# RMS norm factors applied behind the products: gated projection, latent attention and final rows of a two-layer decoder step

## The reference, cut to what matters

```python
def rmsnorm(x, g):
    y = x * rsqrt(mean(x * x, axis=-1) + EPS)      # one factor per token
    return y * g                                   # one gain per channel

# layer 0
h = h + conv_module(rmsnorm(h, g_mix[0]))
h = h + hier_moe(rmsnorm(h, g_ffn[0]), ...)        # 32 experts, two per token
h = ple_add(h, p[0], g_ple[0], ...)
c    = rmsnorm(rmsnorm(h, g_kv_in) @ w_dkv, g_lat) # shared latent, 256 wide
k_pe = rope(rmsnorm(h, g_kv_in) @ w_kr)            # 32 wide
# layer 1
cq = rmsnorm(rmsnorm(h, g_mix[1]) @ w_dq, g_q)     # 384 wide
h  = h + attention(cq, c, k_pe, cache) @ w_o
h  = h + hier_moe(rmsnorm(h, g_ffn[1]), ...)
h  = ple_add(h, p[1], g_ple[1], ...)
y  = rmsnorm(h, g_final)

def ple_add(h, p, g, w_gate, b_gate, w_proj):
    gate = sigmoid(rmsnorm(h, g) @ w_gate + b_gate)  # 1024 x 1024
    return h + gate * (p @ w_proj)                   # 256 x 1024
```

## Time and profile before

| | |
|---|---|
| median of 3 runs | 1585.22 us (1583.94 to 1587.91) |
| profiled execution | 1589.59 us, its span 1587.7 us |
| PE busy | 1201.2 us, 76% of the span |
| DVE busy | 499.3 us, 31% |
| ACT busy | 264.5 us, 17% |
| POOL busy | 58.9 us, 4% |
| mean granted TensorE clock | 0.861 of full speed |
| DMA moved | 477.03 MB |

### The profile page before, as it was taken

The page is one execution under the profiler, slowest core; times in us unless marked ns, Lnnn a source line. Parts: engine busy times, 40 slices in busy tenths (PEclk is TensorE's granted clock), DMA queues, the critical chain, the costliest instruction groups (busy, mean ns, idle before and its releaser), DMA issues. The chain is left out here.

```text
span 1587.7 us, 23342 instructions
## 1 busy us (share of the span) xinstructions
PE 1201.2 (76%) x10176; PEld 781.7 (49%) x10176; DVE 499.3 (31%) x1326; ACT 264.5 (17%) x643; POOL 58.9 (4%) x46
## 2 busy tenths in 40 slices
PE   6978897865866855579898897989776676675586
PEld 4846664433433532347675554855443343343265
DVE  2792512112112112132575664151111111111143
ACT  1162221100100100011223432022000010010011
POOL 0340000000000000000200100000000000000000
PEclk9989998877877877789999998899787787887898
DMA  5953269999999998995213342629999999999930
GB/s 155 296 213 137 106 270 422 418 423 420 418 423 419 419 423 325 416 346 127 106 46 142 132 168 107 258 108 419 422 419 420 422 418 421 421 419 419 418 128 28
DMA packets 91279, 477.03 MB, mean 300 GB/s; under 512 B 21676, under 2 KB 32841, under 8 KB 73230
## 3 DMA queue, kind: packets, MB, share of 16 engines
q1 hardware_dynamic: 89188, 456.34, 71.5%
q0 software_dynamic: 1792, 18.88, 3.2%
q10 hardware_dynamic: 186, 0.20, 0.0%
HBM read 473.37 MB, written 2.49 MB: 300 GB/s over the span
## 5 line engine op out<-in xcount | busy, mean ns | idle before, releaser
L880 PE MATMUL ps<-area,hiddenT 128*32 128x256 f32 x2112 | 201.9, 547 | 236.6 <-issue 223.5
L880 PEld LDWEIGHTS ps<-area,hiddenT 128*32 128x32 f32 x2112 | 92.4, 148 | 319.8 <-issue 299.4
L1452 DVE COPY y<-ps 32x256 f32<-32x256 f32 x128 | 53.3, 417 | 471.9 <-PE ps L880 471.0
L870 PE MATMUL ps<-area,uT 128*32 128x256 f32 x2176 | 148.3, 432 | 42.1 <-DMA area<-in_w_exp_up_dram 27.9
L870 PEld LDWEIGHTS ps<-area,uT 128*32 128x32 f32 x2176 | 84.6, 127 | 105.3 <-issue 44.1
L870 PE MATMUL ps<-area,xsT 128*32 128x256 f32 x2048 | 134.9, 420 | 0.0
L1160 PE MATMUL ps<-sel,u_rows 128*128 128x256 f32 (+3 forms) x480 | 123.6, 384 | 0.0
L1408 ACT COPY y<-ps 32x256 f32<-32x256 f32 x128 | 46.7, 364 | 431.4 <-PE ps L880 430.6
L870 PEld LDWEIGHTS ps<-area,xsT 128*32 128x32 f32 x2048 | 82.6, 126 | 55.3 <-issue 25.7
L1498 DVE TENSOR_TENSOR hidden<-silu,ps 128x128 f32<-128x128 f32 x64 | 18.4, 287 | 266.4 <-ACT silu L1420 266.4
L1160 PEld LDWEIGHTS ps<-sel,u_rows 128*128 128x128 f32 (+1 forms) x480 | 75.7, 188 | 40.7 <-issue 31.8
(11 more groups left out here) (325 smaller groups left out, 1278.6 us busy)
## 6 DMA issues: line engine op xcount, KB each, us to landing
area<-in_w_exp_gate_dram SPq DMA_DIRECT2D x66, 2048.0 KB, 27.1
area<-in_w_exp_up_dram SPq DMA_DIRECT2D x66, 2048.0 KB, 30.6
area<-in_w_exp_down_dram SPq DMA_DIRECT2D x66, 2048.0 KB, 26.1
area<-in_conv_w_in_dram SPq DMA_DIRECT2D x8, 1024.0 KB, 12.7
area<-in_w_ple_gate_dram SPq DMA_DIRECT2D x2, 4096.0 KB, 35.8
area<-in_conv_w_out_dram SPq DMA_DIRECT2D x1, 4096.0 KB, 19.3
area<-in_w_o_dram SPq DMA_DIRECT2D x1, 4096.0 KB, 14.2
area<-in_w_uq_dram SPq DMA_DIRECT2D x3, 768.0 KB, 12.2
```

The source lines that it names most:

```text
L870: last = pe.matmul(s.ps[SLOT * j:SLOT * (j + 1), bank, 0:2 * P].rearrange("p (a f) -> p a f", a=2), xT[:, k, :], up[:, :, k, j * P:(j + 1) ...
L880: last = pe.matmul(s.ps[SLOT * g:SLOT * (g + 1), bank, 0:q], hidden[:, SLOT * j:SLOT * (j + 1)], down[:, j, g * q:(g + 1) * q], start=(j = ...
L1452: last = V.tensor_copy(y[a:a + SLOT, (e // PER) % 2, g * q4:(g + 1) * q4], s.ps[SLOT * g:SLOT * (g + 1), 3 + e % 2, 0:q4])
```

## The change

1. Norm factors behind the products. For the gate product of `ple_stage`, the latent, rotary and query products of `mla_stage` and the final rows, only the gain is applied before the product, by ACT (`Copy` with a scale per partition). The factor per token is multiplied onto each product's result by DVE. For the final rows the gained chunks are turned into rows first and the factor, turned too, is applied as a scale per partition while the rows are copied out.
2. Chunk by chunk. Gain and square of a chunk follow the add that completes it in `hT`: those for the gate product behind the last `combine` within the experts' block, those of the next norm behind each chunk of the gate, with the sum of squares (and in layer 1 the transposes) placed on PE between the gate products.
3. The per-layer products `p @ w_proj` move into experts 28 to 31, two chunks per expert, copied by ACT into `m.proj`, which takes the room of `u_rows`. Squares and gained chunks lie in the room of the down slots.
4. `final_stage` is gone; its work stands in layer 1's `ple_stage`. The output goes out in three DMAs, one of them issued by ACT. `w_ple_proj` has a semaphore of its own.

The diff, cut to its core (the loops of ACT and DVE over the chunks of `ple_stage` are whole):

```diff
 # experts_stage, PE
+                def project(c):
+                    if c == 0:
+                        pe.wait_ge(s.ple_proj_in.sem, s.ple_proj_in.at(16))
+                    else:
+                        pe.wait_ge(s.ple_out.sem, s.ple_out.at(c))
+                    for k in range(PLE // P):
+                        last = pe.matmul(s.ps[:, 5, 0:T], ple_weights(s)[1][:, k, c * P:(c + 1) * P],
+                                         s.pT[:, layer, k, :], start=(k == 0), stop=(k == PLE // P - 1))
+                    last.then_inc(s.ple_mm.sem, 1)
...
+                    if e >= CUT:
+                        project(2 * (e - CUT))          # behind the transpose of expert e
...
+                    if e >= CUT:
+                        project(2 * (e - CUT) + 1)      # behind its down product
 # experts_stage, ACT, behind the last expert
+                for c in range(DC):
+                    act.wait_ge(s.added.sem, s.added.at(DC * (quads - 1) + c + 1))
+                    gain = VEC["g_ple"] + DC * layer + c
+                    nc.scalar.activation(s.uT[:, c, :], s.hT[:, c, :], ACT.Copy, scale=s.vec[:, gain:gain + 1])\
+                        .then_inc(s.gained.sem, 1)
 # experts_stage, DVE, behind the last expert
                 for c in range(DC):
                     add(quads - 1, c)
+                    if c:
+                        square(c - 1)
+                square(DC - 1)
 # ple_stage, PE
+                pe.wait_ge(s.ple_in.sem, s.ple_in.at(16))
+                gate_products(0)
+                for c in range(DC):
+                    mm = sum_of(c)
+                mm.then_inc(s.sums.sem, 1)
+                for c in range(1, DC):
+                    gate_products(c)                    # waits for scaled(c - 2) from c = 2 on
+                    if c >= 2:
+                        followed(c - 2)                 # sum_of(c - 2); in layer 1 also turn_rows(c - 2)
+                followed(DC - 2)
+                followed(DC - 1)
+                if last:
+                    pe.wait_ge(s.rooted.sem, s.rooted.at(2))
+                    for i, (t0, n) in enumerate(TILES):
+                        turned = pe.transpose(s.ps[0:n, 0, i * P:(i + 1) * P], s.rstd[:, t0:t0 + n], col(s, "ident"))
+                    turned.then_inc(s.pe.sem, 1)
 # ple_stage, ACT
+                act.wait_ge(s.sums.sem, s.sums.at(1))
+                root(nc, s, s.rstd, sums, D).then_inc(s.rooted.sem, 1)
+                for c in range(DC):
+                    act.wait_ge(s.scaled.sem, s.scaled.at(c + 1))
+                    nc.scalar.activation(gate[:, c % 2, :], gate[:, c % 2, :], ACT.Sigmoid, ...)
+                    act.wait_ge(s.proj_out.sem, s.proj_out.at(c + 1))
+                    for at, dst in gains:               # two in layer 0, one in layer 1
+                        gained = nc.scalar.activation(dst[:, c, :], s.hT[:, c, :], ACT.Copy, ...)
+                    gained.then_inc(s.gained.sem, 1)
+                    if last and c == 4:
+                        act.wait_ge(s.rows_turned.sem, s.rows_turned.at(4))
+                        nc.scalar.copy(y[0:NB, 2, 0:512], s.ps[0:NB, 3, :]).then_inc(s.rows_out.sem, 1)
+                if last:
+                    act.wait_ge(s.sums.sem, s.sums.at(2))
+                    root(nc, s, s.rstd, sums, D).then_inc(s.rooted.sem, 1)
+                    act.wait_ge(s.inverted.sem, s.inverted.at(2))
+                    for half in range(2):
+                        out = nc.scalar.activation(y[:, 1, 512 * half:512 * half + 512], s.ps[:, 6 + half, :], ACT.Copy,
+                                                   scale=per_row[:, 1:2])
+                    act.dma_start(io["out_y_prompt"][0, P:SEQ], y[:, 1, :]).then_inc(s.stores.sem, 16)
 # ple_stage, DVE
+                V.reciprocal(s.rstd[:], s.rstd[:]).then_inc(s.inverted.sem, 1)
+                for c in range(DC):
+                    dve.wait_ge(s.proj_mm.sem, s.proj_mm.at(c + 1))
+                    V.tensor_tensor(gate[:, c % 2, :], s.ps[:, c % 2, 0:T], s.rstd[:], ALU.mult)   # scaled
+                    dve.wait_ge(s.acted.sem, s.acted.at(c + 1))
+                    link(V.tensor_tensor(gate[:, c % 2, :], gate[:, c % 2, :], m.proj[:, c, :], ALU.mult))
+                    V.tensor_tensor(s.hT[:, c, :], s.hT[:, c, :], gate[:, c % 2, :], ALU.add)      # proj_out
+                    V.tensor_tensor(v.squares[:, c, :], s.hT[:, c, :], s.hT[:, c, :], ALU.mult)    # squared
+                if last:
+                    V.reciprocal(per_row[:, 0:2], s.ps[:, 0, 0:2 * P:P])
+                    V.reciprocal(per_row[0:NB, 2:3], s.ps[0:NB, 0, 2 * P:2 * P + 1]).then_inc(s.inverted.sem, 1)
+                    for half in range(2):
+                        out = V.tensor_scalar(y[:, 0, 512 * half:512 * half + 512], s.ps[:, 4 + half, :],
+                                              per_row[:, 0:1], None, ALU.mult)
...
 # mla_stage
-            norm.squares_on_act()
-            norm.root_on_act(act)
-            for c in range(DC):
-                last = nc.scalar.activation(mixed[:, c, :], s.hT[:, c, :], ACT.Copy, ...)
+            root(nc, s, s.rstd, 3, D).then_inc(s.rooted.sem, 1)
...
-            for c in range(DC):
-                G_.tensor_tensor(mixed[:, c, :], mixed[:, c, :], s.rstd[:], ALU.mult).then_inc(s.second.sem, 1)
...
-            return lambda V_, bank, link: V_.tensor_copy(dst[:, c, :], bank[:, 0:T])
+            return lambda V_, bank, link: V_.tensor_tensor(dst[:, c, :], bank[:, 0:T], s.rstd[:], ALU.mult)
```

More of the change, by code:

```diff
@@ L1580, in _ @@
             def _(pe):
-                def project(m):
-                    if m >= 4:
-                        pe.wait_ge(s.proj_out.sem, s.proj_out.at(m - 3))
-                    for k in range(PLE // P):
-                        pe.matmul(s.ps[:, 4 + m % 4, 0:T], proj[:, k, m * P:(m + 1) * P],
-                                  s.pT[:, layer, k, :], start=(k == 0), stop=(k == PLE // P - 1))
-                norm.sums(pe)
-                pe.wait_ge(s.ple_in.sem, s.ple_in.at(32))
-                for m in range(4):
-                    project(m)
@@ L1593, in _, with gate_products @@
[L1593 to L1603 removed]
+                def gate_products(c):
+                    if c >= 2:
+                        pe.wait_ge(s.scaled.sem, s.scaled.at(c - 1))
+                    for k in range(DC):
+                        mm = pe.matmul(s.ps[:, c % 2, 0:T], w[:, k, c * P:(c + 1) * P], s.uT[:, k, :],
+                                       start=(k == 0), stop=(k == DC - 1))
+                    mm.then_inc(s.proj_mm.sem, 1)
@@ L1617, in _ @@
             @block.vector
             def _(dve):
[L1619 to L1620 removed]
+                V = nc.vector
                 link = chained(dve, s.dve)
[L1622 to L1627 removed]
@@ L1629, in ple_stage @@
+        s.ple_in.ended(16)
         s.proj_mm.ended(DC)
         s.proj_out.ended(DC)
+        s.scaled.ended(DC)
         s.acted.ended(DC)
+        s.gained.ended(DC)
+        s.squared.ended(DC)
+        s.sums.ended(2)
+        s.rooted.ended(2 if last else 1)
+        s.inverted.ended(2 if last else 1)
         s.dve.ended(DC)
```

214 lines of the change are left out of this document (117 added, 97 removed).

## The result

The changed kernel takes 1557.86 us (median of 4 runs, 1556.84 to 1561.67). The kernel before, run beside it, takes 1584.73 (median of 4, 1583.94 to 1587.91). The ratio is 0.9831, 95% interval 0.981 to 0.9853: 26.9 us faster, where 20.6 were predicted.

What follows compares the result with a forecast made beforehand. DMA bytes bound the two expert stages, unchanged; between and behind them the norm chains decide. Layer 0 -13.1, layer 1 -11.2 and clock +3.7 sum to -20.6, from 1585.2 to 1564.6 us; range 1559.5 to 1571.5.

Steps and rivals of the forecast that it cites:

- Squares beside the combine: Behind the last expert, DVE's adds and squares take 7.3 us where the adds took 4.6: +2.7 per layer.
- the tail: Layer 1, last gate product to the end: 11.3 us instead of 22.1, saving 10.8.
- The clock at the gate products: PE idles about 2.3 us ahead of the gate products, bringing one half-clock spell: +1.7 in each layer.
- Rival A: The clock does not fall at the gate products, since a half-busy combine may suffice: 1560.9 us, chance 0.30.
- The clock at the latents: End of layer 0's gate stage: +0.3 for a gap of 2.0 us broken by one sum.
- The latents at full clock: Layer 0's latent and query products, 50 matmuls, take 22.4 us instead of 25.9: -3.5.
- The per-layer products: In experts 28 to 31 they are mostly hidden by DMA waits; expert 31 leaves +0.4 per layer.
- the ring: Expert-weight DMAs issued up to 1.6 us later, but the queue's backlog keeps it from running dry: price 0.
- no PE wait for `scaled`: Gate products: chunk 0 is scaled by 9.9 to 10.3 us, before PE ends chunk 1 at 10.7.
- Rival B: DVE and the stores are dearer: add waits, sample DMA last, a third half-clock spell; 1569.9 us, chance 0.12.
- C: Layer 0's 9.6 us up to the latents is lost to waits for dq matrix or page table: 1574.2, chance 0.05.
- D: Slower: a whole gate stage stays at half clock, some 33 us more, 1597.6 us; chance 0.03.

Runs made afterwards that it cites:

- experiment 2: Changed kernel with each of the 8 squares behind the last combine computed twice, in both layers: 1568.27 us, ratio 0.989.
- experiment 9: Changed kernel with only the squares of chunks 6 and 7 computed twice beside the combine, in both layers: 1563.08 us, ratio 0.9867.
- experiment 3: Changed kernel with the 8 squares moved behind the adds, beside the first gate products: 1558.34 us, ratio 0.9829.
- experiment 7: Kernel before with only the per-layer products moved into experts 28 to 31, norms as they were: 1575.77 us, ratio 0.9943.
- run 1: The changed kernel once more, no edit: 1561.06 us, ratio 0.9855.
- run 4: Changed kernel with the per-layer products put back into the gated projection, all 16 matmuls ahead of the gates: 1573.37 us, ratio 0.9922.
- run 5: Changed kernel with the attention's norm in layer 0 done as in the kernel before: 1566.29 us, ratio 0.9878.
- experiment 6: Changed kernel with layer 1's final norm, transposes, copies and stores in the old stage, as before: 1566.69 us, ratio 0.9871.

## Why the prediction was wrong

- **Squares beside the combine: the step that failed.** "DVE has 16 operations of 0.44 with a wait each, 0.455, 7.3 us: +2.7." It took 5.77. The 0.44 is how long one operation lasts; the next independent one starts 0.34 after its start (0.33 and 0.34 per operation in experiments 2 and 9, 8 in 2.84 in 3). A wait on a semaphore that has been reached costs nothing here: each of the 16 has one. The Trainium skill (VectorE: DVE Perf Modes, The DRAIN you can't avoid) says that the next operation waits until the pipe has emptied, and adds that one which is not held starts earlier; the trace shows the second, a start 0.08 ahead of the shown end. The distance is 0.47 only where the next reads what the one before wrote, as from 1544.90 to 1545.37 in the tail. The trace of before had it, in the first norm's squares on DVE:

```profile
705.96 1.46 DVE L433 TENSOR_TENSOR ple_squares<-hT 128x264 f32<-128x264 f32 x4 [0.33 <-PEq L1238]
```

  Four in 1.46 is 0.43 + 3 x 0.34, and I read the two adds in 0.88 instead, which PE paced. By experiment 3 the squares' price in the whole stretch is 0.65 instead of 2.7, and the start of the gates without them saves 7.15 (13.34 - 6.19) instead of 7.5: together -1.7 per layer against the prediction, 3.4 in both.
- **The clock at the gate products** (+1.7 per layer) followed from that step. The rule behind it, a gap of 2.3 us brings a spell of 1.7, held in experiment 9 and not in experiment 7; but the gap was 1.6. That is 3.4 more, and in part luck: at 1.6 the clock fell in 3 of 14. Rival A was right in its outcome, not in its reason: it took the gap for 2.3 us too and held the half-busy combine before it to be enough, and experiment 9 has that combine, that gap and the fall.
- **The clock at the latents** was priced too low: +0.3, where a spell of 1.7 came in 5 of 9 profiled executions of this form. On the average 0.9.
- **The latents at full clock** take 22.8 (run 1) and not 22.4. With the spell of 1.7 that is why -3.5 became -1.3. That the whole 3.5 had been the clock's was wrong too: about 1.6 of it was DVE slowed beside POOL (experiment 7).
- The per-layer products cost nothing instead of +0.4 in each layer; that the ring would not run dry by their delay was right.
- Right as predicted: the streams, +2.3 and +4.0; the last gate to the first latent product, -7.3, with root, table load and reciprocal beside the latents; the attention weights in time; no PE wait for `scaled`; the tail, 11.2 against 11.3, with the table load at 1.29.
- Rival B fell with the squares, which were cheaper; C did not show (from the last combine to the first latent product it was 44.9 us instead of 56.3); D did not (no stage stayed at half clock).

In all: predicted -20.6; squares -3.4, clock at the gates -3.4, latents +1.9 (1.4 by the clock beyond the 0.3, the rest their length at full clock), products in the experts -1.0, tail -0.2, the rest +0.2 make the -26.5 of the table, and the medians say -26.9. What remains is under the spread of the runs.

Put back one by one (experiments 4, 5 and 6, by place, without the spells at the gates) the parts give 14.4, 5.5 and 8.5. That is 28.4 together, of which 1.9 is the later start and the longer transposes of the old norms.

No run undoes the gate product's own norm alone, but the traces allow an estimate. From the combine to the end of the gates a layer took 45.5 before, 41.7 with only the products moved (run 7), 46.3 with only the norm rebuilt (run 4, its extra sums of 2.2 taken off), and 39.1 with both (run 5, which has no extra sums in layer 0). So the rebuilt norm alone would have saved nothing there, since the per-layer products had filled PE's wait for root and reciprocal. Moved out alone they saved 3.8, and both together 6.4.

The range was too narrow as well: two medians of the same kernel lay 3.2 apart, and I had left A's time less than that.

## What to carry to other kernels

Price a row of independent operations by the distance of their starts, not by their length: a row of the trace with a count above one gives both, and only dependent ones pay the full length. Reckon an engine's idle time from that before reckoning with the clock, since 0.7 us of gap changed how often the spell (1.7 us) came: 3 of 14 places at 1.6, 4 of 6 at 2.2 to 2.3. Where a norm's factor is one number per column, it can be applied behind the product, and then squares, sums, root, table load and reciprocal lie beside the product instead of ahead of it. That pays only if PE had nothing else to do in that wait. Matmuls whose inputs are ready early belong into a stage that waits for DMA, where 16 of them (7.2 us) cost nothing.

## What the runs showed of the hardware

- The same code at the same place with the same gaps runs at 0.50 or at 1.00: the latents in 24.52 or 22.83, the sums of the norm in 5.52 or 3.83, the convolution's stage to 122 or to 126. In a kernel of 1560 us this moves single executions by 4 us and more, so a difference between two profiled spans is not the change's (32.7 here, 26.9 by the medians).
- The longer PE had stood ahead of a stretch of dense products, the oftener the clock fell in it. Over all traces, counting stretches of at least 14 records of 264 columns: in none of 47 places at 1.2 to 1.5 us, 3 of 14 at 1.6, 4 of 6 at 2.2 to 2.3, 33 of 48 at 2.7 to 3.0, all 13 at 3.6. Most of these are the same few places in 13 executions. The places differ beyond the gap: behind 2.94 us the router's product fell in 13 of 13 in layer 0 and in 7 of 13 in layer 1. What else decides, the runs don't tell.
- DVE starts the next independent 128x264 operation 0.34 us after the one before it, though each is shown with 0.43.
- A DVE `scalar_tensor_tensor` on 128x264 is shown with 0.49 us (starts 0.40 apart) while POOL is idle, and with 0.97 (0.89 apart) while POOL multiplies tiles of the same shape (run 7).
